# Products with the high parts of freshly split rows ahead of those with the low parts, in a two-block transformer kernel

## The reference

```python
def first_block(x, ...):                      # layers 0 and 1 of the kernel
    for l in range(2):
        proj = x @ w_in[l]
        ... o_a = hgrn2_mixer(...); o_b = nsa_mixer(...)
        mix = jnp.concatenate([o_a, o_b], axis=-1) @ w_out[l]
        x = layer_norm(ALPHA * x + mix, ln1_g[l], ln1_b[l])
        ffn = (jax.nn.silu(x @ w_ffn_gate[l]) * (x @ w_ffn_up[l])) @ w_ffn_down[l]
        x = layer_norm(ALPHA * x + ffn, ln2_g[l], ln2_b[l])

def second_block(x, ...):                     # layers 2 and 3 of the kernel
    for layer in range(2):
        h = rmsnorm(x, attn_norm[layer])
        ... mixed = attention of h @ w_in
        x = x + mixed @ w_o[layer]
        h = rmsnorm(x, ffn_norm[layer])
        x = x + conv_ffn(h, w_up, conv_w, conv_b, w_down)   # (silu(gate) * val) @ w_down
    return rmsnorm(x, final_norm)
```

## Time and profile before

| | |
|---|---|
| median of 3 runs | 1459.33 us (1455.19 to 1459.44) |
| the profiled execution, its own time | 1456.39 us |
| its span, first to last instruction | 1454.6 us |
| mean granted TensorE clock in the span | 0.981 |
| PE busy | 1386.1 us, 95% of the span |
| DVE busy, ACT busy | 958.9 us, 721.4 us |
| HBM traffic | 159 GB/s over the span |

### The profile page before, as it was taken

How to read it: one execution, slowest core, us unless ns; L and a number is a source line. 1 busy time by engine, 2 the same in 40 slices (tenths; PEclk the granted TensorE clock), 3 DMA queues, 4 the chain that set the end, 5 groups by cost and what they waited for, 6 DMA issues and landing times.

```text
span 1454.6 us, 24532 instructions
## 1 busy us (share of the span) xinstructions
PE 1386.1 (95%) x10006; PEld 1282.9 (88%) x10006; DVE 958.9 (66%) x1630; ACT 721.4 (50%) x1199; POOL 85.0 (6%) x79
## 2 busy tenths in 40 slices
PE   9998989999999898999998999999999999999997
PEld 7997789999899777999988899889998999889996
DVE  5666775555759567655565696587777555686776
ACT  4755443333475643433444545555545554555454
POOL 0321000000014100000000002130000000000000
PEclk9998999999999999999998999999999999999999
DMA  8742145555443313655534434345454533445541
GB/s 311 280 155 87 62 152 193 188 189 178 154 190 121 112 59 114 219 189 178 199 116 159 141 121 145 123 158 201 175 185 164 193 118 138 161 156 206 188 174 58
DMA packets 38631, 233.22 MB, mean 160 GB/s; under 512 B 5016, under 2 KB 8808, under 8 KB 12152
## 3 DMA queue, kind: packets, MB, share of 16 engines
q1 hardware_dynamic: 36456, 224.18, 43.5%
q0 software_dynamic: 2064, 7.47, 1.5%
HBM read 230.55 MB, written 1.09 MB: 159 GB/s over the span
## 4 chain that ended last, share of the span: by engine, by line
PE 83%; DVE 8%; ACT 5%; issue 2%; POOL 1%; DVEq 0%; ACTq 0%; POOLq 0%
PE bank L769 24%; PE bank L770 24%; PE bank L771 24%; PE bank L873 2%; DVE w_lo L604 2%; ACT w_hi L594 1%; PE bank L953 1%; PE bank L975 1%; PE bank L977 1%; PE bank L976 1%; DVE a_lo L625 1%; PE bank L798 1%; PE bank L849 1%; DVE arena L1679 0%; ACT a_hi L620 0%
## 5 line engine op out<-in xcount | busy, mean ns | idle before, releaser
L604 DVE TENSOR_TENSOR w_lo<-raw,w_hi 128x1024 fp32r<-128x1024 f32 x404 | 484.8, 1237 | 97.4 <-ACT w_hi L594 94.3
L769 PE MATMUL bank<-a_hi,w_hi 128*128 128x256 f32 x1856 | 531.0, 286 | 3.1 <-DVE w_lo L604 3.1
L770 PE MATMUL bank<-a_lo,w_hi 128*128 128x256 f32 x1856 | 526.7, 284 | 0.0
L771 PE MATMUL bank<-a_hi,w_lo 128*128 128x256 f32 x1856 | 526.6, 284 | 0.0
L594 ACT ACTIVATE w_hi<-raw 128x1024 fp32r<-128x1024 f32 x404 | 406.3, 1050 | 95.7 <-PE bank L771 87.4
L769 PEld LDWEIGHTS bank<-a_hi,w_hi 128*128 128x128 f32 x1856 | 357.5, 193 | 7.6 <-issue 4.5
L770 PEld LDWEIGHTS bank<-a_lo,w_hi 128*128 128x128 f32 x1856 | 357.6, 193 | 1.2
L771 PEld LDWEIGHTS bank<-a_hi,w_lo 128*128 128x128 f32 x1856 | 357.6, 193 | 0.0
L769 PE MATMUL bank<-w_hi,a_hi 128*128 128x256 f32 (+1 forms) x512 | 166.7, 326 | 15.3 <-DVE a_lo L625 15.1
L770 PE MATMUL bank<-w_lo,a_hi 128*128 128x256 f32 (+1 forms) x512 | 160.2, 313 | 0.0
L771 PE MATMUL bank<-w_hi,a_lo 128*128 128x256 f32 (+1 forms) x512 | 160.2, 313 | 0.0
(11 more groups left out here) (252 smaller groups left out, 1487.3 us busy)
## 6 DMA issues: line engine op xcount, KB each, us to landing
raw<-in_stream SPq DMA_DIRECT2D x201, 1024.0 KB, 4.8
bias_t<-bias_rows SPq DMA_DIRECT2D x6, 512.0 KB, 7.6
heads_buf<-in_w SPq DMA_DIRECT2D x2, 1024.0 KB, 8.2
gains<-in_w SPq DMA_DIRECT2D x2, 1024.0 KB, 10.2
gains<-in_ln_g POOLq DMA_DIRECT2D x4, 512.0 KB, 3.9
gains<-in_ln_b POOLq DMA_DIRECT2D x4, 512.0 KB, 5.6
gains<-in_rms_g POOLq DMA_DIRECT2D x3, 512.0 KB, 4.2
res<-in_xT SPq DMA_DIRECT2D x4, 256.0 KB, 5.1
```

The source lines that it names most:

```text
L604: dve.tensor_tensor(w_lo[:, i % PARTS, half_tile(h)], raw[:, i % SLOTS, half_tile(h)], w_hi[:, i % PARTS, half_tile(h)].bitcast(F32), ALU. ...
L769: pe.matmul(out, lh, rh, start=first, stop=False)
L770: pe.matmul(out, lh, rl, start=False, stop=False)
L771: return pe.matmul(out, ll, rh, start=False, stop=last)
```

## The change

Nothing is added to or taken from the arithmetic. Where rows were split freshly, the matmuls of a group are put in another order, and the one wait ahead of the group becomes two: a new helper, `high_first`, issues all products with the high part of the rows, then calls `ready()`, which awaits the low part, and then issues those with the low part. For xT and oT the first wait is on `a_hi_done`, which ACT counts; the second is the old wait. For hidden rows DVE counts a new semaphore, `h_hi_done`, behind `h_hi`, and the first of the four `add_rows` of every down awaits high and low parts of `kk` 0, then those of `kk` 1.

```diff
+            def high_first(out, tiles, ready, first=True, last=True):
+                for i, ((lh, _), (rh, rl)) in enumerate(tiles):
+                    pe.matmul(out, lh, rh, start=first and i == 0, stop=False)
+                    pe.matmul(out, lh, rl, start=False, stop=False)
+                ready()
+                for i, ((_, ll), (rh, _)) in enumerate(tiles):
+                    mm = pe.matmul(out, ll, rh, start=False, stop=last and i == len(tiles) - 1)
+                return mm
+
+            def wait_high(key):
+                pe.wait_ge(a_hi_done, turned_no[key] + X_PARTS + 1)
...
-                for k in range(KT):
-                    if norm is not None and k % 4 == 0:
-                        wait_drained(pe, (norm, "xT", tt, k // 4))
...
+                for q in range(2):
+                    turned = (norm, "xT", tt, q)
+                    wait_high(turned)
+                    mm = high_first(out, tiles[4 * q:4 * q + 4], lambda: wait_drained(pe, turned), q == 0, q == 1)
                 return mm
...
-            def add_rows(key, left, tt, hf, first, last):
+            def add_rows(key, left, tt, hf, first, last, high=None, low=None):
...
+                elif low is None:
+                    for kk in range(2):
+                        high(kk, h_hi_done)
+                        mm = high_first(out, tiles[kk:kk + 1], lambda: high(kk, h_done), first and kk == 0,
+                                        last and kk == 1)
+                else:
+                    high()
+                    mm = high_first(out, tiles, low, first, last)
...
             def add_output(l, r, tt, hf):
-                wait_drained(pe, (l, "oT", r))
+                high, low = lambda: wait_high((l, "oT", r)), lambda: wait_drained(pe, (l, "oT", r))
...
-                        pe.wait_ge(h_done, l * FT + 2 * j + 2)
...
-                                add_rows((l, f"down{j}"), hidden(j), tt, hf, j == 0, False)
+                                add_rows((l, f"down{j}"), hidden(j), tt, hf, j == 0, False,
+                                         hidden_ready(l, j) if tt == hf == 0 else None)
...
-                step(dve.tensor_scalar(h_hi[:, j % HSLOTS, :], full, 1.0, None, ALU.mult))
+                dve.tensor_scalar(h_hi[:, j % HSLOTS, :], full, 1.0, None, ALU.mult).then_inc(h_hi_done, 1)
+                dve.wait_ge(h_hi_done, l * FT + j + 1)
```

More of the change, by code:

```diff
@@ L494, in build @@
         silu_done = sem("silu_done")
+        h_hi_done = sem("h_hi_done")
         h_done = sem("h_done")
@@ L784, in tokens @@
                 t = slice(tt * P, (tt + 1) * P)
-                for k in range(KT):
-                    if norm is not None and k % 4 == 0:
-                        wait_drained(pe, (norm, "xT", tt, k // 4))
-                    mm = products(b[:, tt * S:(tt + 1) * S], (a_hi[:, k, t], a_lo[:, k, t]),
-                                  [part[:, k, :] for part in w], k == 0, k == KT - 1)
+                tiles = [((a_hi[:, k, t], a_lo[:, k, t]), [part[:, k, :] for part in w]) for k in range(KT)]
+                out = b[:, tt * S:(tt + 1) * S]
+                if norm is None:
+                    for k in range(KT):
+                        mm = products(out, *tiles[k], k == 0, k == KT - 1)
+                    return mm
+                for q in range(2):
+                    turned = (norm, "xT", tt, q)
+                    wait_high(turned)
+                    mm = high_first(out, tiles[4 * q:4 * q + 4], lambda: wait_drained(pe, turned), q == 0, q == 1)
                 return mm
@@ L1010, in turn_outputs @@
                 close_bank(mm)
-            def add_rows(key, left, tt, hf, first, last):
+            def add_rows(key, left, tt, hf, first, last, high=None, low=None):
                 w = [part.rearrange("p (k c) -> p k c", k=2) for part in weights(key)]
[L1015 to L1019, removed]
+                out = bank[:, 4 + 2 * tt + hf, :]
+                tiles = [([part[:, kk, tt * P:(tt + 1) * P] for part in left],
+                          [part[:, kk, hf * 512:(hf + 1) * 512] for part in w]) for kk in range(2)]
+                if high is None:
+                    for kk in range(2):
+                        mm = products(out, *tiles[kk], first and kk == 0, last and kk == 1)
+                elif low is None:
+                    for kk in range(2):
+                        high(kk, h_hi_done)
[4 more added lines that the diff above has]
+                    mm = high_first(out, tiles, low, first, last)
                 if last:
@@ L1023, in add_rows, with hidden_ready @@
                     mm.then_inc(rows_used, 1)
+            def hidden_ready(l, j):
+                return lambda kk, part_done: pe.wait_ge(part_done, l * FT + 2 * j + kk + 1)
             def add_output(l, r, tt, hf):
-                wait_drained(pe, (l, "oT", r))
+                high, low = lambda: wait_high((l, "oT", r)), lambda: wait_drained(pe, (l, "oT", r))
                 if r == 0:
                     wait_drained(pe, before_output(l, 4 + 2 * tt + hf))
-                add_rows((l, f"out{r}"), mixed_part(l, r), tt, hf,
-                         r == 0, r == 3)
+                add_rows((l, f"out{r}"), mixed_part(l, r), tt, hf, r == 0, r == 3, high, low)
             def rest_of_output(l):
@@ L1044, in add_tail @@
                             x_transposes(norm, 0)
-                        if tt == 0:
-                            pe.wait_ge(h_done, l * FT + 2 * (FT // 2 - TAIL + i) + 2)
                         for hf in range(2):
-                            add_rows(key, left, tt, hf, False, i == TAIL - 1)
+                            add_rows(key, left, tt, hf, False, i == TAIL - 1,
+                                     hidden_ready(l, FT // 2 - TAIL + i) if tt == hf == 0 else None)
                 if norm == 4:
```

## The result

The changed kernel takes 1451.33 us (median of 8 runs, 1446.47 to 1455.39), the kernel before 1459.32 (8 runs, 1455.09 to 1460.28): ratio 0.995, 95% interval 0.9934 to 0.9966, so 5 to 10 us faster. 1447 was predicted, between 1442 and 1454. The direction and the range hold; of the 10.3 us forecast, about 8 are there.

The account below looks back on a forecast made before the run. The prediction took matmuls on PE to bound the kernel, with only PE's idle time to win: 1.44 + 4.2 + 2.3 + 2.4 = 10.3 us, giving 1447 us, between 1446.1 and 1449.0 from two bases; range 1442 to 1454.

Parts of the forecast that it names:

- Part 1: First output products (oT), layers 0 and 1: PE starts 0.72 us earlier in each, 1.44 us won.
- Part 2: Normalised rows (xT), token half 1: PE starts 0.72 us earlier at five places, 0.6 at another; 4.2 us won.
- Part 3: xT, token half 0, three places: PE starts earlier but then waits for DVE's norm of half 1; nothing won.
- Part 4: First down, layers 2 and 3: PE is through with the group 1.16 us earlier in each; 2.3 us won.
- Part 5: Last down, layers 2 and 3: the stall and the slow start behind it go, 1.2 us each; 2.4 us won.
- Costs: About 255 more waits on PE and low products one behind another, all costed at nothing.
- the absorbed case: Rival, 16%: DVE or ACT sets the pace, Part 1 and Part 2 bring nothing; 4.7 us won, 1452 to 1453.
- The rival that stretches at the lower clock vanish with the shorter stalls: Rival, 14%: two half-clock stretches at Part 1 and one or two more vanish; 13.7 to 17 us won, 1440 to 1443.
- signs by which the prediction called itself wrong: DVE or ACT waits behind moved products taking back gains, matmuls visibly carrying added waits, or granted clock moving over 0.002.

Follow-up runs that it names:

- lean: The changed kernel with token half 0 and all downs but the last three back in the old form; 1452.47 us, ratio 0.9945 to the kernel before.
- all_parts: The changed kernel itself, timed again beside its separate parts on one chip; 1450.57 us, ratio 0.9935 to the kernel before.
- xt_only: The changed kernel with output products and downs back in the old form, only normalised rows (xT) split; 1456.10 us, ratio 0.998 to the kernel before.
- more_waits: The kernel before with 264 redundant waits added on PE, order unchanged; 1460.89 us, ratio 0.9998 to the kernel before.

## Why the prediction was right where it was, and wrong where it was

**Part 1 (oT), 1.44 us forecast, 0.9 measured.** Both stalls shrank by 0.63, to 2.33 where 2.2 were worked out. About 0.3 us of each came back as a longer wait for `x` at the next norm, an entry of the earlier trace rows that the prediction called not touched. That leaves some 0.6 us by the traces; the timing says 0.9, with an error of 0.35.

**Part 2 (xT, token half 1), 4.2 forecast, 3.6 measured.** Right, by mechanism and nearly by size. Its stalls are 0.34 us.

**Part 3 (token half 0, costed at nothing).** Right in size, but the cover is for the most part another one. PE starts 0.73 us earlier, and lean, without this part, loses nothing by it. The forecast had PE wait 0.72 us longer for the `res` rows at 941.59; it is 0.06 (0.34 to 0.40). PE stops sooner, at 938.09, ahead of the second weight tile. The 0.45 us there have no releaser in the view, but DVE's split of that tile ends at 935.64 + 2.35 = 937.99:

```profile
935.64 2.35 DVE L605 TENSOR_TENSOR w_lo<-raw,w_hi 128x1024 fp32r<-128x1024 f32 x2
```

PE starts 0.10 behind it, where four low products from 937.00 on, at 0.12 each, would have let it go on at 937.48. That the wait is for this split is read from the times and from the order in the program. In layer 3 (split done at 1256.54, PE at 1256.64), in all_parts and in xt_only it is 0.10 again. Before, the split was done at 933.99 and PE took up the tile at 934.21: with the 0.10 for the release that is 0.12 us in hand, and the other 0.61 of the 0.73 were lost to it. PE's wait for the `res` rows as a whole grew from 6.0 us to 8.0 in one profile of the changed kernel, but only to 6.4 in the other (all_parts), and this says little.

**Part 4 (first down), 2.3 forecast, 0.3 measured. This step failed.** It ended the working at the group, "PE is through with the group at 961.71", and took the end of the group for the end of the effect. I asked what PE waits for next only at token half 0, where a wait stood in the list. Behind the first down none was listed, though the split of the next weights already set PE's start there, 0.15 us behind its end, in layer 2 (966.98 and 967.13) and in layer 3 (1287.10 and 1287.25). Any earlier arrival of PE had to turn into a wait for `w_lo`, and it did, of 1.05 us in each layer. Of the 18 such places in the nine profiles with the old wait, twelve have this same 0.15; at the other six PE comes 1.5 to 1.7 us behind the split's end, in lean because the clock drops right behind the stall (0.67 from 961 to 965). There the tie would let a gain through, and no run singles that out. The profile of before held these rows. The gain up to the end of the group was there: in layer 3 the stall went from 1.83 to 0.68. The 2.2 us forecast for `h_hi` in layer 2 came out at 1.52, because the stall of 3.29 in the profile of before was a long one; seven of the eight other profiles with the old wait have 2.67 to 2.76 there. The two shorter waits for `w_lo` that are also new in the list of the changed kernel (0.60 us at 12.34 and 0.42 at 594.38) are not the change's: more_waits has them too, with 0.57 and 0.41.

**Part 5 (last down), 2.4 forecast, 2.2 measured.** Right in the stall, 1.12 us in each layer. The 0.1 for the slow start behind it did not come: at 1118.20 no stall stands, and the next matmul still starts 0.34 us later, at 1118.54. The two layers' stalls alone are 2 x 1.12 = 2.24.

**Costs, nothing forecast.** Right: +0.5 us for 264 waits and -0.2 us for the order, with errors of 0.3. That is at most some 4 ns for a wait.

**The sum.** With part 4 at 0.3, the forecast's terms give 1.44 + 4.2 + 0.3 + 2.4 = 8.3 us, and the measured ones 0.9 + 3.6 + 0.3 + 2.2 = 7.0, with 7.2 for the whole and 8.0 by the two medians. The 1451.33 us are 4.3 above the 1447 forecast: 2.3 because less was won, 2.0 because the kernel before ran at 1459.3 and not at the 1457.3 from which 1447 was counted. They lie just outside the 1444 to 1451 that the forecast gave as its own. The range of 1442 to 1454 held because it was drawn out for rivals, and in part by luck: the absorbed case names parts 1 and 2 and keeps part 4, and it was part 4 that was absorbed.

**The clock.** The rival that stretches at the lower clock vanish with the shorter stalls is not shown, and not wholly excluded. The changed kernel's mean clock was 0.9796 over its first 8 runs and 0.9809 over 12 more; that of before was 0.9790 over 89. Over all 20 that is 0.0014 more, with an error of 0.0007 to 0.0008; but lean, with the same stalls shortened at token half 1, the output products and the last downs, had 0.9779 over 9. The forecast that 0.002 of clock would be 3 us is borne out: the slope gives 2.7. Two of the signs by which the prediction called itself wrong did appear: DVE waits behind the moved products took back a part (parts 1, 3 and 4), and the clock of the profiled execution moved by 0.004, which single executions of one kernel do by themselves.

## What to carry to other kernels

A stall that shrinks is worth what the next tie to another engine lets through. So look, behind each place, for the waits that are met by a hair, not only for those that are listed: take the end of each operand's producer and the start of its first reader, and take off what a release takes (0.10 to 0.15 us here). The smallest difference that is left is the most that can be won upstream. Await the part of an operand that the next instructions read, and put the ones that need less first: a wait that is already met cost nothing that could be measured on TensorE here. And where single runs differ by more than the effect, compare them at equal granted clock before believing or dismissing a per cent.

## What the runs showed of the hardware that was not expected

The time of one kernel moves with the clock that an execution happens to be granted. The kernel before ran between 1451.86 and 1467.35 us in 89 runs, the changed one between 1443.65 and 1459.09 in 12 on one chip. The clock of the runs lay between 0.973 and 0.986 in all eleven kernels and that of before, and the slope of 1.36 us for 0.001 explains nearly all of it. That is close to what the levels give: 0.001 of clock over 1458 us is 2.9 us at 1.2 GHz in place of 2.4 GHz, and half of that, 1.46 us, is lost where PE sets the pace. The first matmul of 512 columns behind a stall is followed by the next only after 0.34 us in place of 0.23 (961.38 and 961.72 in the earlier trace rows). It is not the stall alone that does this: at 1118.20 the stall is gone and the distance is still 0.34. What makes it stays open.
